# A two-layer float32 transformer block on one core: high and low activations streamed as one 512-column matmul, with the two bank halves added when they are read

## What is computed

```python
n = rms_norm(x, attn_norm_g)
proj = n @ w_in                                   # stages conv, rest
g_qkv = silu(causal_short_conv(g_qkv, w))         # 16 of the 45 tiles of proj
h = x + concat([gla_out, nsa_out]) @ w_out        # stage out
m = rms_norm(h, ffn_norm_g)
x = h + (silu(m @ w_gate) * (m @ w_up)) @ w_down  # stages up0, down0, up1, down1, up2, down2
mod = silu(c) @ mod_w + mod_b                     # shift, scale, gate; for c and for c_ctx
...                                               # stages ev_kv, ev_q, ev_z, ev_out: attention layer
y = concat([outA, outB]) * silu(z);  x = x + gate * rms_norm(y @ w_out, post_g)
y = pooled(u) * silu(z);             x = x + gate * rms_norm(y @ w_out, post_g)   # od_u, pool, od_z, od_out
```

## Time and profile before

| | us |
|---|---|
| three runs | 2448.59, 2452.38, 2456.30 |
| median | 2452.38 |
| span of the profiled execution | 2443.0 |
| PE busy / PEld busy | 2199.2 / 2127.6 |
| DVE busy / ACT busy | 1576.2 / 995.4 |
| mean granted TensorE clock | 0.920 |

### The profile page before, as it was taken

The page is one execution under the profiler, slowest core; times in us unless marked ns, Lnnn a source line. Parts: engine busy times, 40 slices in busy tenths (PEclk is TensorE's granted clock), DMA queues, the critical chain, the costliest instruction groups (busy, mean ns, idle before and its releaser), DMA issues.

```text
span 2443.0 us, 45011 instructions
## 1 busy us (share of the span) xinstructions
PE 2199.2 (90%) x16718; PEld 2127.6 (87%) x16718; DVE 1576.2 (65%) x2077; ACT 995.4 (41%) x1230; POOL 0.2 (0%) x4
## 2 busy tenths in 40 slices
PE   5999987489799999999999996999689998888997
PEld 5999986369799999999999985999378998888997
DVE  5888564548787577764767576346656766666544
ACT  4346631333355632343333344223245633424642
POOL 0000000000000000000000000000000000000000
PEclk8999966569899999999999997999699998998998
DMA  4767521007567586765878682357003875444552
GB/s 174 245 239 270 184 80 44 0 1 241 172 220 236 174 287 227 263 226 186 269 259 273 200 294 85 100 181 273 6 1 127 271 248 171 138 138 142 185 181 95
DMA packets 119530, 433.76 MB, mean 178 GB/s; under 512 B 13216, under 2 KB 13600, under 8 KB 119216
## 3 DMA queue, kind: packets, MB, share of 16 engines
q1 hardware_dynamic: 119472, 432.98, 53.2%
HBM read 430.83 MB, written 2.10 MB: 177 GB/s over the span
## 4 chain that ended last, share of the span: by engine, by line
PE 69%; DVE 16%; DMA 8%; issue 4%; ACT 2%; SPq 1%; DVEq 1%; ACTq 0%
PE ps L411 19%; PE ps L413 19%; PE ps L412 19%; DMA side<-w_side 8%; DVE w_lo L1002 3%; PE ps L643 2%; PE ps L473 2%; PE ps L468 1%; DVE sq L1064 1%; PE ps L480 1%; DVE mod_sum L1014 1%; DVE at_max L1339 1%; PE ps L512 1%; PE ps L437 1%; PE ps L632 1%
## 5 line engine op out<-in xcount | busy, mean ns | idle before, releaser
L411 PE MATMUL ps<-a_hi,w_hi 128*128 128x256 f32 x3280 | 939.8, 287 | 58.4 <-DVE w_lo L1002 33.4
L412 PE MATMUL ps<-a_lo,w_hi 128*128 128x256 f32 x3280 | 934.2, 285 | 0.0
L413 PE MATMUL ps<-a_hi,w_lo 128*128 128x256 f32 x3280 | 933.8, 285 | 0.0
L776 ACT ACTIVATE w_hi<-raw 128x1024 fp32r<-128x1024 f32 x610 | 634.2, 1056 | 699.3 <-PE ps L413 636.0
L1002 DVE TENSOR_TENSOR w_lo<-raw,w_hi 128x1024 fp32r<-128x1024 f32 x610 | 718.8, 1220 | 108.3 <-ACT w_hi L776 105.6
L411 PEld LDWEIGHTS ps<-a_hi,w_hi 128*128 128x128 f32 x3280 | 635.8, 194 | 66.1 <-DVE w_lo L1002 35.5
L412 PEld LDWEIGHTS ps<-a_lo,w_hi 128*128 128x128 f32 x3280 | 636.0, 194 | 0.0
L413 PEld LDWEIGHTS ps<-a_hi,w_lo 128*128 128x128 f32 x3280 | 635.8, 194 | 0.0
L411 PE MATMUL ps<-b_hi,w_hi 128*128 128x256 f32 x1664 | 485.0, 291 | 17.6 <-DVE w_lo L1002 8.4
L413 PE MATMUL ps<-b_hi,w_lo 128*128 128x256 f32 x1664 | 473.8, 285 | 0.0
L412 PE MATMUL ps<-b_lo,w_hi 128*128 128x256 f32 x1664 | 473.7, 285 | 0.0
(11 more groups left out here) (242 smaller groups left out, 1462.6 us busy)
## 6 DMA issues: line engine op xcount, KB each, us to landing
raw<-w_main SPq DMA_DIRECT2D x610, 512.0 KB, 4.3
side<-w_side SPq DMA_DIRECT2D x200, 512.0 KB, 5.6
x_tok<-x_in SPq DMA_DIRECT2D x4, 512.0 KB, 6.0
ctx_tok<-ctx_tok SPq DMA_DIRECT2D x1, 2048.0 KB, 9.2
y_out<-o_tok SPq DMA_DIRECT2D x4, 512.0 KB, 2.7
cons<-cons_in SPq DMA_DIRECT2D x1, 542.0 KB, 8.0
table<-counts_tab SPq DMA_DIRECT2D x1, 512.0 KB, 10.1
table<-masks_in SPq DMA_DIRECT2D x1, 448.0 KB, 11.1
```

Of the source, the lines that this page charges most:

```text
L411: pe.matmul(out_ap, wh, act_hi[:, kt, :], start=first and n == 0, stop=False)
L412: pe.matmul(out_ap, wh, act_lo[:, kt, :], start=False, stop=False)
L413: mm = pe.matmul(out_ap, wl, act_hi[:, kt, :], start=False, stop=last and n == len(blocks) - 1)
L776: act.activation(w_hi[:, slot, :], raw[:, slot, :], ACT.Copy).then_inc(hi_ready, 1)
```

## The change

The high and low activations now lie behind each other in one buffer (`a_act`, `b_act`), so that one matmul with `w_hi` streams both, 512 columns, into a whole PSUM bank: columns 0 to 255 get w_hi·a_hi, columns 256 to 511 get w_hi·a_lo. The matmul with `w_lo` adds its 256 columns onto the first half. So a block has two weight loads and two matmuls, where it had three and three, of 768 columns in all as before. Only the pool stage keeps three.

The two halves of a bank must be added. VectorE takes one of its operands from PSUM, so ACT copies the upper half to `half` in SBUF first (new, once a step, twice in ev_kv), and tells `half_ready`; DVE waits for that where it waited for `halves_used`. Its copy becomes an addition of the two (`sum_halves`). Where it did more than copy, it has one instruction more: the convolution first sums into `conv_u`, `res` is added to twice, and in the up and z stages the sum goes to `pre`. ACT's silu reads `pre` and waits for DVE's sum of that step (`dve_read`), where it read PSUM and waited for PE. `dve_reads` now counts every step, and PE may start any step s when step s-2 has been summed.

```diff
+            def half_products(bank, c, par, blocks, act, first, last, split=None):
...
-                    pe.matmul(out_ap, wh, act_hi[:, kt, :], start=first and n == 0, stop=False)
-                    pe.matmul(out_ap, wh, act_lo[:, kt, :], start=False, stop=False)
-                    mm = pe.matmul(out_ap, wl, act_hi[:, kt, :], start=False, stop=last and n == len(blocks) - 1)
+                    pe.matmul(ps[:, bank, :].rearrange("p (a t) -> p a t", a=2), wh, act[:, :, kt, :],
+                              start=first and n == 0, stop=last and n == len(blocks) - 1, skip_group_check=True)
+                    mm = pe.matmul(ps[:, bank, 0:T], wl, act[:, 0, kt, :], start=False,
+                                   stop=last and n == len(blocks) - 1, skip_group_check=True)
...
-                    step(stage, i, k, (a_hi, a_lo), free=(silu_ready, i * 2 + (FFN_TILES + done + k)))
+                    step(stage, i, k, a_act, free=(dve_read, i * 2 + (FIRST[stage] + k - 1)))
...
 -                act.wait_ge(halves_used, i * 4 + (2 * s + 2))
+                act.wait_ge(dve_read, i * 2 + (FIRST[stage] + k + 1))
                 act.wait_ge(S("gate_y"), i + (silus + 1))
-                act.activation(sg[:, 0, :], ps[:, s % 2, 0:T], ACT.Silu).then_inc(silu_ready, 1)
+                act.activation(sg[:, 0, :], pre[:, 0, :], ACT.Silu).then_inc(silu_ready, 1)
...
                  def body(i, k):
-                    if FIRST[stage] + k + 1 < STEPS:
-                        hi(i, FIRST[stage] + k + 1)
+                    s = FIRST[stage] + k
+                    if s + 1 < STEPS:
+                        hi(i, s + 1)
+                    act.wait_ge(halves_used, i * 4 + (2 * s + 2))
+                    if stage == "ev_kv":
+                        act.activation(half_c[:, s % 2, :], ps[:, 2 + s % 2, T:2 * T], ACT.Copy)
+                    act.activation(half[:, s % 2, :], ps[:, s % 2, T:2 * T], ACT.Copy).then_inc(half_ready, 1)
                     if extra is not None:
                         extra(i, k)
                     if squared is not None and k:
...
-                    dve.wait_ge(halves_used, i * 4 + (2 * s + 2))
+                    before = s if s < FIRST["od_z"] else s - COUNT["pool"]
+                    dve.wait_ge(half_ready, i * 2 + (before + 1))
                     read(i, k, s % 2)
...
+            def sum_halves(dst, bank):
+                return dve.tensor_tensor(dst, psum_tile(bank), half[:, bank:bank + 1, :], ALU.add)
...
-                    dve.tensor_copy(tile(dst, i, k + k0), psum_tile(bank)).then_inc(dve_read, 1)
+                    sum_halves(tile(dst, i, k + k0), bank).then_inc(dve_read, 1)
...
-                dve.tensor_tensor(tile(res, i, k), psum_tile(bank), tile(res, i, k), ALU.add).then_inc(dve_read, 1)
+                    dve.tensor_tensor(tile(res, i, k), psum_tile(bank), tile(res, i, k), ALU.add)\
+                       .then_inc(S("res_part"), 1)
+                    dve.wait_ge(S("res_part"), i * 2 + (before + k + 1))
+                    dve.tensor_tensor(tile(res, i, k), half[:, bank:bank + 1, :], tile(res, i, k), ALU.add)\
+                       .then_inc(dve_read, 1)
...
+                    sum_halves(pre[:, k % 2:k % 2 + 1, :], bank).then_inc(dve_read, 1)
                     if k % 2:
-                        split_out(i, 1, done + k // 2, psum_tile(bank), k // 2)
+                        dve.wait_ge(dve_read, i * 2 + (FIRST[f"up{c}"] + k + 1))
+                        split_out(i, 1, done + k // 2, pre[:, 1:2, :], k // 2)
...
+                    sum_halves(pre[:, 0:1, :], bank).then_inc(dve_read, 1)
                     other = tile(pr, i, k + k0)
                     split_out(i, 2, FFN_TILES + done + k, other, k)
```

96 lines of the change are left out of this document (51 added, 45 removed).

## The result

| | before | after |
|---|---|---|
| median of four runs each, us | 2454.34 | 2530.74 |
| lowest to highest | 2448.59 to 2464.99 | 2525.39 to 2534.77 |
| span of the profiled execution | 2443.0 | 2523.6 |
| mean granted TensorE clock | 0.920 | 0.919 |

After / before is 1.0321, with a 95% interval of 1.0285 to 1.0358 (the two medians of the table divide to 1.0311): slower by 3.2%, where 3.4% was forecast. The question is where 80.6 us of span came from. The page of the changed kernel first: busy times, the chain by engine, then two groups (busy us, mean ns of one, idle time before them and its releaser).

The account below looks back on a forecast made before the run. Mostly PE bounds the kernel; loops through DVE and the side transfer hold some stages. -36 + 64 + 38 + 7 + 11 = +84 us on 2443.0, plus 9.4 from span to median: 2536 us, range 2490 to 2575.

Parts of the forecast that it names:

- PE's gain where PE holds the step: In 173 steps held by PE, a pair of matmuls takes 347 ns for 360, 0.21 us a step: -36 us.
- the square behind the copy: In out, ev_out, od_out (53 us) and down2 (11), ACT's square waits behind the new copy and stalls PE: +64 us.
- silu behind the sum: In up and z stages ACT's silu waits for DVE's sum behind the side add, so ACT joins the loop: +38 us.
- conv and down0: Longer reads by DVE: the sum behind conv's side add, +4 us, and down0's second addition to `res`, +3.
- ends, od_u, od_z: Copy plus sum delay what follows a stage's last tile in some 12 places, +8 us; od_u and od_z +3.
- B: Rival: the long matmul covers the weight load, 336 ns a pair, -66 us in place of -36, 2507 us; chance 0.30.
- C: Rival: reading the activations is the limit, 360 ns a pair, no gain, 2572 us; chance 0.17.
- E: Rival: not slower; the rate of loads alone holds the 120 ns, deciding from 317 ns a pair, 2448 us; chance 0.03.
- D: Rival: every matmul takes its columns and 2.5 ns, 325 ns a pair, 2475 us; chance 0.05.
- The stall: In stages of squares, last matmul to sum of squares takes 1.2 us where it was 0.12: 1.1 us a step.
- W: Wait for the side half in loops through DVE and the side transfer: taken as 6.5 us, ends 6.2 and 6.9.
- Covered: ACT's copies, 305 x 0.38 = 116 us, lie in its idle time elsewhere and make nothing late.

Follow-up runs that it names:

- PE's part alone: Kernel before, with the 512 and 256 column matmuls but no copy and no sum, upper bank half left out of the result: 2418.70 us, 0.9855 of before.
- the second trace: The changed kernel with nothing altered, measured and profiled again beside later runs: 2538.02 us.
- the first trace: The first profiled execution of the changed kernel, span 2523.6 us, from its first measurement, median 2530.74 us.
- the run with the square first: Changed kernel, with ACT's square of tile s-1 issued ahead of the wait for step s and the copy: 2497.78 us, 1.0172 of before.
- The run without table loads: Changed kernel, with a plain copy for the silu in up0 to up2, ev_z and od_z: 2508.72 us.
- the one with the sum ahead: Changed kernel, with DVE's sum ahead of the side addition in z stages and even steps of up stages: 2515.09 us, 1.0231 of before.

## Why the prediction was right, and where it was not

**Where the time went.** The mechanism held: what PE saves is earned in few stages, and an order on ACT and one on DVE cost more. Term by term, against the traces of before and after:

| | forecast | measured |
|---|---|---|
| PE's gain where PE holds the step | -36 | -31.5 (PE's part alone), 15 to 23 in the finished kernel |
| the square behind the copy | +64 | +52 by the stages, some 48 with what comes back behind out |
| second addition to `res` in down2 | 0 | +4 |
| silu behind the sum, ev_z | +17 | +15.6 |
| the same in the first half of up0, with its lead | +16 | +13.8 |
| the same in up1, up2 | +5 | +2.6 |
| conv and down0 | +7 | +3.3 (9.0 in the second trace) |
| ends, od_u, od_z | +11 | +5 |
| attention part at the half clock | 0 | +7.9 |
| span in all | +84 | +80.6 |

The measured terms come from different executions and overlap by some us, so they don't add up exactly. That the total is 3.4 us from the forecast is in part luck: the square, the ends, conv and down0 cost some 22 us less than forecast, and a smaller gain of PE, down2's second addition and the attention part, which the forecast had at 0, make up for most of it; the three stages of squares by themselves grew by 41.7 us, PE's gain in them included, where the forecast's terms make 40.

**The pair.** 227 + 120 = 347 ns was called, and the reason, 13 ns that come once with each matmul and its load at the full clock, is what the lengths 256, 384 and 512 show. What failed is the step from the reason to the rate: with alternating lengths only part of the steps reaches 347, 176 of some 300 stand at 353.3 in the first trace, and the mean over the kernel is 350. 173 steps of 16 blocks x 10 ns are 28 us in place of 36. Rivals B (336) and C (360), on which 0.47 of the chance lay, are ruled out, so is E, which needed 317 or less, and so is D: the Trainium skill, TensorE: Matmul & The Clock Gate, section Back-to-back issue gap, has N / 2.4 + 2.5 ns for isolated matmuls, and at each of three lengths the traces here have N / 2.4 + 13.3 for this type with a load for each matmul.

**The stall.** The chain from the last matmul to the sum of squares was put at 1.2 us, and 1.06 is there, 0.94 more than before and not 1.1. What fills it up is a term that the forecast did not have: the load of the sum of squares is no longer hidden, so that PE needs 0.349 us from it to the next matmul in place of 0.246, and 0.56 in about every other step. A step of out at 7.12 us against a forecast of 7.1 is right with one term too large and one missing. In down2 the forecast put +11 on the square; the run with the square first took 2.5 of it away and left 4.4. The likely cause of the rest is the second addition to `res` in the loop with the side transfer; no run takes it away by itself, but the kernels without it there took 82.2 to 85.1 us, against 87.0 and 87.5. The forecast counted that addition in down0 and forgot it here, and took PE for the limit of the step where the loop was. Its 0.42 for the sum of squares is right (a step of out took 6.18 before), but its "100.0" would give 0.49, and W in conv comes out as 7.1 and not 6.9 by its own terms; neither changes the sum by more than 1 or 2 us.

**The silu.** Loops of 14.3 and 13.6 us for two steps were forecast in up0 and ev_z, 14.5 and 14.0 are there. The run without table loads confirms that they are in the loop, the one with the sum ahead that the side half is. The forecast did not see that PE begins up0 some 9 us earlier and loses it in the first pair (21.1 us against 13.1).

**Covered.** That 116 us of copies cost nothing in themselves holds where they are off these two orders: in down1 and ev_q PE is busy 90.50 of 90.50 and 88.80 of 88.80 us, and with three matmuls beside the same copies both take 92.2 us, as before the change.

**The span and the median.** The 9.4 us between span and median were carried over as if fixed. A run's time is its span and 1.8 us (2525.39 for the profiled 2523.6); the rest was that the profiled execution of before was at its fast end. For after the median stood 7.1 us above the span too, so the step did no harm, by luck.

**Ends.** They cost about half of the 11 us. But the attention part from rest to out, which the change does not touch, grew from 231.2 to 239.1 us. The clock accounts for it. Windows over about the same matmuls of the attention, before:

```profile
406.00:416.00 10.00, 9.31 (x72) 8.54 (x71) 0.00 (x0) 3.67 (x5) 0.00 (x0) 0.96 0.00 0
```

and after:

```profile
400.00:412.00 12.00, 12.00 (x59) 12.00 (x58) 0.00 (x0) 1.61 (x3) 0.00 (x0) 0.50 0.00 0
```

A stretch in which PE is the limit had the full clock before (0.96) and has the half clock, 1.2 GHz, after (0.50), though the mean granted clock of the whole attention part reads 0.63 in both. The half clock fell at other moments, and it lasted 178.8 us in place of 169.9. Why it did is not shown. The part took 233.9 to 243.6 us in the traces of all other kernels here, so the one trace of before has the lowest value of them. That this execution lay 7.6 us below the median of before fits this, but with one trace of before it is not shown.

## What to carry to other kernels

A wider matmul that saves a matmul and its weight load is worth 7 to 13 ns at the full clock, nothing where PE waits, and it needs an engine to bring the halves together: give it only to the stages that PE holds, and put the wait for PE's end behind everything on that engine that is ready before it. An instruction that waits should stand last, and a sum that another engine waits for should stand ahead of any wait for a transfer. A stage measured by PE alone can look faster than it is: when PE's steps become shorter than those of the engine that reads its results, the lag comes back behind the stage. Before a forecast takes single stages to a few us, it should know how much they vary from one execution to the next; here conv and down0 stood 4 us apart and the attention part up to 12 between kernels that don't differ in them, and 2 to 4 us between two executions of the changed kernel, as much as most of the gains.

## What the runs showed of the hardware

- fp32r matmuls that each have a load of their own start 13.3 ns and their columns at 2.4 GHz apart: 120.0, 173.3, 226.7 ns for 256, 384, 512 columns. At 128 columns it is 111.7 ns, most likely the pace of the loads. The Trainium skill, on the same page in its section LDWEIGHTS (loading the stationary operand), puts a load at its columns divided by 1.2 GHz, 107 ns for 128, which this is near to.
- Alternating 512 and 256 columns, PE falls into one of two rhythms when such a stretch starts, 346.7 or 353.3 ns a block, and stays in it until it is interrupted. Two and two, or 512, 256, 256, 512, took 348.3 in all twenty runs.
- From the start of the float32 sum of squares to the next matmul PE takes 0.349 us or more when it had to wait for the data, and 0.246 when the weights were loaded ahead.
- Which matmuls of the attention part meet the half clock differs between kernels that don't differ in this part: it lasted 169.9 us of 231.1 in the trace of before and 178.8 of 238.9 in that of after, 8 us more for the part, though the mean clock reads 0.63 in both.
